# Attention's weighted sums: from one fp32 product to three fp32r products of high and low halves

## What is computed

```python
logits = (jnp.einsum('bhqn,bhkn->bhqk', qb, kh).astype(jnp.float32) * scale
          + cqb[..., None] - ck[:, :, None, :])
mask = key_pos[None, :] <= q_pos[:, None]
logits = jnp.where(mask, logits, -jnp.inf)
p = jax.nn.softmax(logits, axis=-1)
return jnp.einsum('bhqk,bhkn->bhqn', p.astype(vh.dtype), vh)
```

## Time and profile before

| | |
|---|---|
| median of 3 runs | 1924.19 us (1923.52 to 1924.32) |
| the profiled execution | 1921.38 us |
| its span, first to last instruction | 1919.6 us |
| mean granted TensorE clock | 0.977 |
| PE / PEld / DVE / ACT / POOL busy | 1836.2 / 1596.3 / 977.6 / 946.9 / 431.8 us |

### The profile page before, as it was taken

How to read it: one execution, slowest core, us unless ns; L and a number is a source line. 1 busy time by engine, 2 the same in 40 slices (tenths; PEclk the granted TensorE clock), 3 DMA queues, 4 the chain that set the end, 5 groups by cost and what they waited for, 6 DMA issues and landing times.

```text
span 1919.6 us, 55790 instructions
## 1 busy us (share of the span) xinstructions
PE 1836.2 (96%) x24271; PEld 1596.3 (83%) x24271; DVE 977.6 (51%) x1873; ACT 946.9 (49%) x1712; POOL 431.8 (22%) x425
## 2 busy tenths in 40 slices
PE   6899999999999999999798999999999999999898
PEld 5798989898998989998698778888888888887676
DVE  7456665666666665666433652534344444344521
ACT  6455454545555554544323525364645555555621
POOL 2223142423323242421000321212121213111010
PEclk8999999999999999999799989999999999999899
DMA  6101010100101010101242110111111101111334
GB/s 234 45 11 45 6 52 9 45 16 28 31 19 42 6 52 9 52 9 30 85 147 103 46 34 16 35 29 28 29 28 29 38 24 39 28 29 28 99 100 136
DMA packets 103735, 89.85 MB, mean 47 GB/s; under 512 B 4101, under 2 KB 95864, under 8 KB 103240
## 3 DMA queue, kind: packets, MB, share of 16 engines
q1 hardware_dynamic: 99544, 66.41, 11.9%
q0 software_dynamic: 3168, 17.14, 2.8%
q10 hardware_dynamic: 784, 2.76, 0.4%
HBM read 64.96 MB, written 21.33 MB: 45 GB/s over the span
## 4 chain that ended last, share of the span: by engine, by line
PE 88%; DVE 5%; ACT 3%; issue 2%; DMA 1%; POOL 0%; SPq 0%; DVEq 0%; ACTq 0%; POOLq 0%
PE ps L1951 8%; PE ps L2563 7%; PE ps L1952 6%; PE ps L2460 6%; PE ps L1953 6%; PE ps L2461 6%; PE ps L2462 6%; PE ps L1877 3%; PE ps L2043 3%; PE ps L1879 3%; PE ps L1878 3%; PE ps L2062 3%; PE ps L2534 2%; PE ps L2506 2%; PE ps L2535 2%
## 5 line engine op out<-in xcount | busy, mean ns | idle before, releaser
L1951 PE MATMUL ps<-xh,wh 128*128 128x258 f32 (+1 forms) x1024 | 320.5, 313 | 4.1 <-ACT arena L1045 2.7
L1952 PE MATMUL ps<-xh,wl 128*128 128x258 f32 (+1 forms) x1024 | 291.6, 285 | 0.0
L1953 PE MATMUL ps<-xl,wh 128*128 128x258 f32 (+1 forms) x1024 | 291.1, 284 | 0.0
L2460 PE MATMUL ps<-xh,wh 128*128 128x348 f32 x744 | 254.5, 342 | 3.3 <-ACT arena_b L1305 3.3
L2461 PE MATMUL ps<-xh,wl 128*128 128x348 f32 x744 | 240.1, 323 | 0.0
L2462 PE MATMUL ps<-xl,wh 128*128 128x348 f32 x744 | 239.8, 322 | 0.0
L1822 DVE TENSOR_REDUCE arena_b<-ps 128x1 f32<-128x144 f32 (+4 forms) x224 | 106.2, 506 | 205.6 <-PE ps L2510 171.7
L1951 PEld LDWEIGHTS ps<-xh,wh 128*128 128x128 f32 x1024 | 193.8, 189 | 16.7 <-ACT arena L1045 4.6
L1952 PEld LDWEIGHTS ps<-xh,wl 128*128 128x128 f32 x1024 | 194.5, 190 | 1.9
L1953 PEld LDWEIGHTS ps<-xl,wh 128*128 128x128 f32 x1024 | 193.6, 189 | 0.0
L1014 ACT ACTIVATE arena<-ps,pp 128x257 f32<-128x257 f32 (+1 forms) x128 | 61.3, 479 | 227.2 <-PE ps L1953 227.2
(11 more groups left out here) (298 smaller groups left out, 4476.6 us busy)
## 6 DMA issues: line engine op xcount, KB each, us to landing
wr<-in_w_in SPq DMA_DIRECT2D x33, 512.0 KB, 4.5
xt_scr<-arena POOLq DMA_DIRECT2D x2, 4176.0 KB, 13.0
wr<-in_kv_w SPq DMA_DIRECT2D x16, 512.0 KB, 4.0
wr<-in_b_w_in SPq DMA_DIRECT2D x16, 512.0 KB, 3.9
arena<-xt_scr SPq DMA_DIRECT2D x8, 522.0 KB, 4.6
arena<-oa_scr SPq DMA_DIRECT2D x8, 520.0 KB, 4.5
wr<-in_w_out SPq DMA_DIRECT2D x8, 512.0 KB, 5.2
ob_scr<-arena_b POOLq DMA_DIRECT2D x16, 256.0 KB, 2.9
```

The costliest lines, as they stand in the source:

```text
L1951: pe.matmul(bank, wh[:, j, k, :], xh[:, k, t], start=(k == 0), stop=False)
L1952: pe.matmul(bank, wl[:, j, k, :], xh[:, k, t], start=False, stop=False)
L1953: mm = pe.matmul(bank, wh[:, j, k, :], xl[:, k, t], start=False, stop=(k == KO - 1))
L2460: pe.matmul(bank[:, 0:SEG], wh[:, slot, k, :], xh[:, k, t], start=(k == 0), stop=False)
```

## The change

P and V are each split into a high half, rounded to fp32r, and a low half, the rest. The product becomes three fp32r products: high V by high P, low V by high P, high V by low P. For P, ScalarE takes two exponentials of the score bank, the first into fp32r (L1348 of the new code), the second into a float32 buffer (L1352, two buffers now), and VectorE subtracts (L1827). TensorE's first two products wait for the first, its third for the subtraction. The second exponential is also the one that TensorE's next scores wait for, and it waits itself for the subtraction two units earlier. The halves of P lie in weight slots 2 and 3 (`p_store`), for the last head in `ka`, `qa`, `kb2`, `qb2` of head 0. For V, ScalarE copies the transposed rows to a float32 place (`v_rows`, in `bsq`), then to fp32r (L1328), and VectorE subtracts (L1819). Some semaphores of the forget gate are merged, an unused table of ones isn't filled, and two memsets change their targets.

```diff
         at[0] = 0
         kb, qb, zb, vb, bsq, brs, zg = (carve_b(TP) for _ in range(7))
-        vflat = [carve_b(NT * P).rearrange("p (t x) -> p t x", t=NT) for _ in range(2)]
-        pt = [carve_b(512) for _ in range(4)]
+        pt = [carve_b(512) for _ in range(2)]
...
+        v_rows = bsq[:, 0:NT * HD]
...
+        p_store = [a[:, 2:4, :, :].rearrange("p s k c -> p (s k c)") for a in (wh, wl)]
+        p_last = ((ka[0], qa[0]), (kb2[0], qb2[0]))
...
                 if j:
                     act.wait_ge(S.b_done, chunk(p, L_SK) + 3)
+                if p >= 0:
+                    act.wait_ge(S.v_lo, 2 * p + 2)
                 act.activation(bsq, (kb, qb)[j], ACT.Square).then_inc(S.hn_sq, 1)
...
                         act.wait_ge(S.b_done, chunk(p, local) + 1)
-                        if p + e > 0:
-                            act.wait_ge(S.pv_done, NU * (2 * p + 1 - e))
...
+                            act.wait_ge(S.b_evac, chunk(p, local) + 1)
+                            if p + e > 0:
+                                act.wait_ge(S.pv_done, NU * (2 * p + 1 - e))
+                            act.activation(vhi[:, :, v_cols(e)], rows_v, ACT.Copy).then_inc(S.v_hi, 1)
...
                             if n_ >= 4:
                                 act.wait_ge(S.pv_done, n_ - 3)
-                            act.activation(pt[n_ % 4][0:n_k, 0:n_q], ps[0:n_k, B_ST[i], 0:n_q], ACT.Exp,
+                            act.activation(p_part(n_, 0)[0:n_k, 0:n_q], ps[0:n_k, B_ST[i], 0:n_q], ACT.Exp,
+                                           scale=SCALE).then_inc(S.p_hi, 1)
+                            if n_ >= 2:
+                                act.wait_ge(S.p_lo, n_ - 1)
+                            act.activation(pt[n_ % 2][0:n_k, 0:n_q], ps[0:n_k, B_ST[i], 0:n_q], ACT.Exp,
                                            scale=SCALE).then_inc(S.p_exp, 1)
...
+                    elif kind == "vrow" and st_[2]:
+                        e = st_[1]
+                        rows_v = v_rows.rearrange("p (t c) -> p t c", c=HD)
+                        dve.wait_ge(S.v_hi, 2 * (p + 1 - e) + e + 1)
+                        dve.tensor_tensor(vlo[:, :, v_cols(e)], rows_v, f32(vhi[:, :, v_cols(e)]),
+                                          ALU.subtract).then_inc(S.v_lo, 1)
+                    elif kind == "scores":
+                        e, g = st_[1:]
+                        for w in GROUPS[g]:
+                            n_k, _, n_q, _, _ = unit(w)
+                            n_ = NU * (2 * p + e) + w
+                            dve.wait_ge(S.p_exp, n_ + 1)
+                            dve.tensor_tensor(p_part(n_, 1)[0:n_k, 0:n_q], pt[n_ % 2][0:n_k, 0:n_q],
+                                              f32(p_part(n_, 0)[0:n_k, 0:n_q]), ALU.subtract).then_inc(S.p_lo, 1)
...
-                            pe.wait_ge(S.p_exp, n_ + 1)
+                            pe.wait_ge(S.p_hi, n_ + 1)
                             if w == 0:
-                                pe.wait_ge(S.b_evac, chunk(p - 1 + e, (L_VROW0, L_VROW1)[e]) + 2)
+                                pe.wait_ge(S.v_lo, 2 * p + e + 1)
...
-                            pe.matmul(ps[:, B_PV[qb_], q0 - 512 * qb_:512], vflat[e][0:n_k, kt, :],
-                                      pt[n_ % 4][0:n_k, 0:n_q], start=(kt == 0), stop=(kt == 4 * qb_ + 4),
+                            o = ps[:, B_PV[qb_], q0 - 512 * qb_:512]
+                            v_h, v_l = (a[0:n_k, kt, e * HD:e * HD + P] for a in (vhi, vlo))
+                            p_h, p_l = (p_part(n_, low)[0:n_k, 0:n_q] for low in (0, 1))
+                            pe.matmul(o, v_h, p_h, start=(kt == 0), stop=False, skip_group_check=True)
+                            pe.matmul(o, v_l, p_h, start=False, stop=False, skip_group_check=True)
+                            pe.wait_ge(S.p_lo, n_ + 1)
+                            pe.matmul(o, v_h, p_l, start=False, stop=(kt == 4 * qb_ + 4),
                                       skip_group_check=True).then_inc(S.pv_done, 1)
```

More of the change, by code:

```diff
@@ L210, in __init__ @@
         self.st_done = sem("st_done")
+        self.v_hi = sem("v_hi")
+        self.v_lo = sem("v_lo")
         self.p_exp = sem("p_exp")
+        self.p_hi = sem("p_hi")
+        self.p_lo = sem("p_lo")
         self.pv_done = sem("pv_done")
@@ L285, in build @@
         EXTRA = slice(HD, HD + 3)
-        ARENA_B = 13848
+        VB = 3 * HD
+        vhi, vlo = (sb(n, [P, NT, VB], F32R) for n in ("vhi", "vlo"))
+        ARENA_B = 10412
         arena_b = sb("arena_b", [P, ARENA_B])
@@ L396, in build, with v_cols, p_part @@
         NU = len(UNITS)
+        v_rows = bsq[:, 0:NT * HD]
+        def v_cols(e):
+            return slice(2 * e * HD, (2 * e + 1) * HD)
+        p_store = [a[:, 2:4, :, :].rearrange("p s k c -> p (s k c)") for a in (wh, wl)]
+        p_last = ((ka[0], qa[0]), (kb2[0], qb2[0]))
+        def p_part(n_, low):
+            i = n_ % 4
+            if n_ // NU == 2 * KO - 1:
+                return p_last[low][i // 2][:, 512 * (i % 2):512 * (i % 2) + 512]
+            return p_store[low][:, 512 * i:512 * i + 512]
         def unit(w):
@@ L860, in _ @@
             pool.wait_ge(S.setup_bp, 8)
-            pool.wait_ge(S.c_hi, 1)
+            pool.wait_ge(S.f_act, 4)
             pool.dma_start(c_scr[:, 0, :], f32(chi[0:H, :])).then_inc(S.c_stored, 16)
-            pool.wait_ge(S.c_lo, 1)
+            pool.wait_ge(S.f_step, 6)
             pool.dma_start(c_scr[:, 1, :], f32(clo[0:H, :])).then_inc(S.c_stored, 16)
@@ L1260, in round_act @@
                     elif kind == "forget":
-                        act.wait_ge(S.f_logit, 1)
-                        act.activation(f_a[0:H, :], f_in[0:H, :], ACT.Abs).then_inc(S.f_abs, 1)
-                        act.wait_ge(S.f_abs, 1)
-                        act.activation(f_a[0:H, :], f_a[0:H, :], ACT.Exp, scale=-1.0).then_inc(S.f_abs, 1)
-                        act.wait_ge(S.f_abs, 2)
-                        act.activation(f_a[0:H, :], f_a[0:H, :], ACT.Ln, bias=1.0).then_inc(S.f_ln, 1)
+                        act.wait_ge(S.f_step, 1)
+                        act.activation(f_a[0:H, :], f_in[0:H, :], ACT.Abs).then_inc(S.f_act, 1)
+                        act.wait_ge(S.f_act, 1)
+                        act.activation(f_a[0:H, :], f_a[0:H, :], ACT.Exp, scale=-1.0).then_inc(S.f_act, 1)
+                        act.wait_ge(S.f_act, 2)
+                        act.activation(f_a[0:H, :], f_a[0:H, :], ACT.Ln, bias=1.0).then_inc(S.f_act, 1)
                     elif kind == "forgotten":
-                        act.wait_ge(S.c_scaled, 1)
-                        act.activation(chi[0:H, :], f_b[0:H, :], ACT.Copy).then_inc(S.c_hi, 1)
+                        act.wait_ge(S.f_step, 5)
+                        act.activation(chi[0:H, :], f_b[0:H, :], ACT.Copy).then_inc(S.f_act, 1)
                     elif kind == "rsq":
@@ L1754, in _ @@
             g = G[N_F % 2]
[L1755 to L1757 removed]
+            dve.tensor_scalar(seg3(f_in[0:H, :]), g[0:H], fb_in[0:H, :], None, ALU.add).then_inc(S.f_step, 1)
+            dve.memset(f32(vhi[:, :, HD:2 * HD]), 1.0).then_inc(S.setup_b, 1)
+            dve.memset(f32(vlo[:, :, HD:2 * HD]), 0.0).then_inc(S.setup_b, 1)
             dve.memset(f_b[0:H, :], 1.0).then_inc(S.setup_b, 1)
@@ L1777, in round_dve @@
                     elif kind == "forget":
-                        dve.wait_ge(S.f_logit, 1)
-                        dve.wait_ge(S.f_abs, 1)
+                        dve.wait_ge(S.f_step, 1)
+                        dve.wait_ge(S.f_act, 1)
                         dve.tensor_scalar(f_in[0:H, :], f_in[0:H, :], 0.0, None, ALU.min).then_inc(S.f_step, 1)
-                        dve.wait_ge(S.f_step, 1)
-                        dve.wait_ge(S.f_ln, 1)
+                        dve.wait_ge(S.f_step, 2)
@@ L1792, in round_dve @@
-                        dve.wait_ge(S.c_lo, 1)
+                        dve.wait_ge(S.f_act, 4)
+                        dve.tensor_tensor(clo[0:H, :], f_b[0:H, :], f32(chi[0:H, :]), ALU.subtract).then_inc(S.f_step, 1)
+                        dve.wait_ge(S.f_step, 6)
+                    elif kind == "vrow" and st_[2]:
+                        e = st_[1]
+                        rows_v = v_rows.rearrange("p (t c) -> p t c", c=HD)
+                        dve.wait_ge(S.v_hi, 2 * (p + 1 - e) + e + 1)
[9 more added lines that the diff above has]
+                                              f32(p_part(n_, 0)[0:n_k, 0:n_q]), ALU.subtract).then_inc(S.p_lo, 1)
```

32 lines of the change are left out of this document (10 added, 22 removed).

## The result

The changed kernel takes **2036.64 us** (median of 4 runs, 2034.4 to 2038.5) against 1923.86 us before on the same chip: ratio 1.0587, 95% interval 1.0568 to 1.0605. It is slower by 5.9%, twice the 54.5 us of the sum and outside the range.

The account below looks back on a forecast made before the run. The prediction took TensorE to bound the kernel: 73.5 us of added waits in seven pairs, plus 5 in the eighth, less 24 saved, gave +54.5 us on 1921.4, and with 2.8 for the median 1979 us; range 1920 to 2010.

Parts of the forecast that it names:

- the sum: Attention rounds: added waits of 73.5 us (seven pairs) and 5 (eighth), less 24 saved on TensorE: +54.5 us.
- (a): First head of a pair, group 1: TensorE waits for low P behind the stackq instructions on VectorE, 3.0 us a pair.
- (d): Second head, group 1: scores 2 wait for the second exponentials, then weighted sums for low P, together 3.6 us a pair.
- (b): First head, fill 3: TensorE's maxima wait for reductions standing behind the subtractions on VectorE, 1.1 us a pair.
- (c): First head, fill 5: late group 5 exponentials, two subtractions and a reduction keep TensorE waiting, 1.8 us a pair.
- (e): Second head, V rows: TensorE waits longer, behind group 3's exponentials on ScalarE and V's halves on VectorE, 1.0 us a pair.
- The clock: Rival: longer idle lowers TensorE's granted clock; given no chance of its own.
- TensorE's saving: Weighted sums: three fp32r products cheaper than one fp32 product, 1.5 us a head, 24 us in all.
- the saving survives: Rival: ScalarE and VectorE run the added work inside TensorE's long fills, leaving about 1900 us; chance 0.15.
- GpSimd's hold: Rival: GpSimd instructions block VectorE's two-operand ones, up to 35 us beyond the sum, about 2014 us; chance 0.05.

Follow-up runs that it names:

- filled run: The change with TensorE multiplying a table of zeros during its longest waits, at group 1 of both heads and the second head's scores 2: 2013.9 us.
- subtractions only: The change with one exponential, straight into high P, and the 224 subtractions as high minus high, TensorE still waiting for them: 1990.7 us.
- no wait for low P: The change with all ScalarE and VectorE work kept, but TensorE's third product reading high P, so not waiting for the subtraction: 2002.6 us.
- the products alone: The change without the second exponential and P's subtractions, the third product reading high P, V's halves kept: 1919.2 us.
- its own run: The change with GpSimd's subtraction for the weights' low halves (L893) made for two of eight channels only: 1992.1 us.

## Why the prediction was wrong

- **The places and the size of the waits: right.** The sum had 73.5 + 5 = 78.5 us; measured are 69.7. By kind it holds too, the forecast for seven pairs, the measured for all eight: low P (a) and (d), 34 us forecast, 29.3 found; reductions (b) and (c), 20 against 23.0 less the 4.9 that stood before; the second exponential in (d), 12 against 16.6 more than before; V rows (e), 7 against 6.2 more. From the third pair on a pair's waits are 10.6 us; in the first two they are shorter, (a) 1.6 and 0.2 us. One place wasn't foreseen: the first head's scores 1 wait 0.78 us for the second exponential. The subtraction was priced a little low: undisturbed it took 0.69 us at 512 columns, against 0.65. The prediction puts that difference at 0.2 us a pair; for twelve of them it is 0.5.
- **The clock: this step failed.** The prediction named it last among its rivals and gave it "no chance of its own", since "the stretch stands at 1.00 and the waits are under 4.5 us apiece". The first half says only that TensorE had been busy without gaps; it couldn't speak for a kernel with gaps. The second half took a length for harmless that no row of before had shown harmless, and the trace of before shows the contrary at the very wait of 2.7 us that the prediction names in the earlier trace rows, in the last pair (TensorE, then two stretches with the columns of the earlier trace rows):

```profile
1778.15 0.70 PE L2506 MATMUL ps<-kb,qc 67*128 67x400 f32 x1 [2.69 <-DVE arena_b L1822]
...
1770.00:1780.00 10.00, 6.36 (x34) 4.40 (x33) 6.71 (x9) 4.84 (x11) 0.00 (x0) 0.80 0.21 61
1780.00:1790.00 10.00, 9.30 (x30) 5.75 (x30) 4.59 (x8) 8.16 (x10) 0.00 (x0) 0.69 0.48 150
```

The granted clock is down to 0.80 and 0.69 there: 10.2 us at the lower level, from 1776.0 us on, within this wait and 2.2 us behind another of 0.95. In the change the added waits brought 103.0 us more at the lower level, 51.5 us of loss. The filled run, in which in the sum this term alone moved, gave its share back. The two don't go in proportion: subtractions only has 61.7 us of waits and 82.9 us at the lower level, no wait for low P 62.9 and 111.9. How the waits lie together seems to decide, which was not tried by itself.
- **TensorE's saving: the term was mis-sized.** 24 us forecast, 5.2 found in the change and 7.1 in the products alone. The price of a product behind another fp32r one (0.23) was right, but behind the bf16 mask the first of a group costs 0.1 more, and about 1.1 of the 1.5 us a head are left, 17 us. This was to be seen in the rows read: L2535 always follows another product of the same shape. From 17 to 7 was not traced to its end. The later start takes 4.5 of it, of which 2.9 are no effect of the change; but a pair of the products alone is only 1.3 us shorter, 10 us in eight, and why it isn't the 2.2 of two heads stays open.
- **Together:** the forecast missed 61.5 us of the span's 116.0: clock 51.5, saving 18.8, waits -8.8. Without the clock it would have been 10 us off, well inside the range. That the waits came out 8.8 us under the forecast and hid some of the saving's miss is luck.
- **The rivals.** That the saving survives would have taken waits under 1 us at (a) and (d). GpSimd's hold was forecast at up to 35 us above the sum. It is real, 45 us in its own run, but a part of it was already in (a), and 23 us of it are the clock behind the waits, which the rival didn't have.
- **What would show it.** The waits for the subtraction are largest at group 1 of both heads: right. PE busy was to be below 92% and is 92.4%, for a slower clock makes busy time too. The weighted sums' 672 products, each counted to the start of the next less the waits, take 141 us, and 130 in the products alone, where 118 were forecast. A pair takes about 106 us, not 97: 9 us too many, of which the clock is 6 to 7.

With everything that the runs found, the change's own work still stands at 1966 us, 2.2% above before. Since the three products alone are worth 5 us, an order of the added work could hardly have made it pay here (argued from that run, not tried for every order), and none of the runs that keep all of the work beats the kernel before. The high half of P as such is cheap; the low half isn't.

## What to carry to other kernels

Where an engine that bounds the kernel runs without gaps, price a new wait twice: its length, and the slow stretch at half clock behind it, which here came to 0.7 us more for each us of wait. An engine at half load is not free room: read where in its queue the new instructions stand, what they delay, and what they wait for, and move them before giving the idea up (70 of 113 us came back by order alone). The price of an instruction read behind its own kind can be too low where kinds alternate; take it from a row that follows the kind it will follow. And before a risk is put at nothing, look in the trace of before for a place where it already occurs: here one wait of 2.7 us with a slow stretch was there to be read.

## What the runs showed of the hardware

- A gap of 2.79 us in TensorE's work, or two of 1.28 and 1.62 us within four, was followed by a stretch at 1.2 GHz, in which a 348-column fp32r product adds 0.29 us instead of 0.16. Behind a gap of 1.35 us it came in one pair of seven, at one of 0.78 us in one of seven too.
- Useless products in the gaps keep part of the clock: 48.2 us less at the lower level for 44.4 us of filler in place of idle time.
- An fp32r product of 512 columns adds 0.22 to 0.24 us behind another fp32r one and 0.32 behind the bf16 mask's; a fp32 one took 0.86. Three of them are 14 to 19% cheaper at 512 columns, at 272 and 144 only 7%.
- One VectorE instruction with two inputs, 1.24 us undisturbed, took 3.41 with a GpSimd one over it, and ended 1.1 us after that one; with GpSimd's made short it took 1.25.
